# Moving the opening of the sample attention stage into the prompt stick-breaking stage

## The reference

```python
z = einsum('bqhd,blhd->bhql', q, k) * HEAD_DIM ** -0.5 + sb_bias[h]
log_1m = where(k_pos < q_pos, log_sigmoid(-z), 0.0)
suffix = cumsum(log_1m, reverse=True) - log_1m
a = where(k_pos < q_pos, exp(log_sigmoid(z) + suffix), 0.0)
o = einsum('bhql,blhd->bqhd', a, v)
# prompt: 1024 queries on 1024 keys, 4 heads of 64
# samples: 64 queries, each on 4096 keys from a paged pool (page_table) and the new rows
```

## Time and profile before

| | |
|---|---|
| times of three runs | 2071.11, 2075.55, 2075.78 us (median 2075.55) |
| span of the profiled execution, first to last instruction | 2072.7 us |
| its own device time | not among the values given; the span is 1.6 us above the shortest run and 2.9 us below the median |
| PE busy in the span | 1904.4 us (92%) |
| DVE, ACT, POOL busy | 995.9, 591.6, 116.1 us |
| prompt stick-breaking | 642.40 to 776.95 us |
| sample stage | 781.86 to about 1083 us |

### The profile page before, as it was taken

How to read it: one execution, slowest core, us unless ns; L and a number is a source line. 1 busy time by engine, 2 the same in 40 slices (tenths; PEclk the granted TensorE clock), 3 DMA queues, 4 the chain that set the end, 5 groups by cost and what they waited for, 6 DMA issues and landing times. The chain is left out here.

```text
span 2072.7 us, 31712 instructions
## 1 busy us (share of the span) xinstructions
PE 1904.4 (92%) x11702; PEld 1612.2 (78%) x11702; DVE 995.9 (48%) x1976; ACT 591.6 (29%) x982; POOL 116.1 (6%) x210
## 2 busy tenths in 40 slices
PE   7999999998787767888877999999999999999996
PEld 6777779998455444565647889999999999999995
DVE  5213441000573854555548455465555546555547
ACT  4221001111854752333323133221231122123113
POOL 0000000000001101232200001000000000000000
PEclk9999999999787877999988999999999999999998
DMA  5444449311715706999945514221021022102102
GB/s 214 170 165 165 170 170 343 125 54 52 174 14 179 254 1 237 341 344 349 335 181 191 189 37 132 62 61 34 26 61 40 21 60 61 37 23 61 41 11 105
DMA packets 134911, 274.09 MB, mean 132 GB/s; under 512 B 23625, under 2 KB 76506, under 8 KB 130778
## 3 DMA queue, kind: packets, MB, share of 16 engines
q1 hardware_dynamic: 113434, 154.33, 22.5%
q0 software_dynamic: 21376, 118.38, 16.1%
HBM read 243.24 MB, written 78.97 MB: 155 GB/s over the span
## 5 line engine op out<-in xcount | busy, mean ns | idle before, releaser
L2032 DVE TENSOR_TENSOR tl_x<-tl_x,tl_ps 128x512 f32<-128x512 f32 (+1 forms) x198 | 135.0, 686 | 195.6 <-PE tl_ps L2247 192.7
L499 PE MATMUL tl_ps<-tl_T_lo,tl_up_hi 128*128 128x364 f32 (+1 forms) x1008 | 222.3, 329 | 0.0
L499 PE MATMUL tl_ps<-tl_T_hi,tl_up_lo 128*128 128x364 f32 (+1 forms) x1008 | 222.3, 329 | 0.0
L499 PE MATMUL tl_ps<-tl_T_hi,tl_up_hi 128*128 128x364 f32 (+1 forms) x1008 | 222.2, 329 | 0.0
L499 PEld LDWEIGHTS tl_ps<-tl_T_hi,tl_up_hi 128*128 128x128 f32 x1008 | 174.9, 188 | 1.4
L499 PEld LDWEIGHTS tl_ps<-tl_T_hi,tl_up_lo 128*128 128x128 f32 x1008 | 174.8, 188 | 0.0
L499 PEld LDWEIGHTS tl_ps<-tl_T_lo,tl_up_hi 128*128 128x128 f32 x1008 | 174.7, 188 | 0.0
L469 PE MATMUL fr_ps<-fr_w_hi,h_hi 128*128 128x512 f32 x384 | 153.9, 401 | 2.6 <-DVE h_lo L365 2.6
L469 PE MATMUL fr_ps<-fr_w_lo,h_hi 128*128 128x512 f32 x384 | 152.5, 397 | 0.0
L469 PE MATMUL fr_ps<-fr_w_hi,h_lo 128*128 128x512 f32 x384 | 152.4, 397 | 0.0
L2247 PE MATMUL tl_ps<-tl_dn_lo,tl_f_hi 128*128 128x512 f32 x360 | 140.3, 390 | 0.0
(11 more groups left out here) (300 smaller groups left out, 3428.7 us busy)
## 6 DMA issues: line engine op xcount, KB each, us to landing
out_s<-in_cache POOLq DMA_DIRECT2D x8, 4080.0 KB, 20.4
all_lead<-in_w_up SPq DMA_DIRECT2D x44, 512.0 KB, 4.6
fr_raw<-in_w_in POOLq DMA_DIRECT2D x9, 2048.0 KB, 8.8
pg_pages<-in_pool SPq DMA_DIRECT2D x64, 256.0 KB, 4.4
pg_pages<-in_pool POOLq DMA_DIRECT2D x64, 256.0 KB, 4.6
sm_pages<-in_pool POOLq DMA_DIRECT2D x64, 256.0 KB, 4.8
sm_pages<-in_pool SPq DMA_DIRECT2D x64, 256.0 KB, 4.7
zs<-fr_zt SPq DMA_DIRECT2D x48, 256.0 KB, 2.0
```

Source lines behind the costliest of these rows:

```text
L499: last = pe.matmul(out[:, n * 512:n * 512 + b - a], lhs, rhs[:, a:b], start=(i == 0), stop=(i == len(pairs) - 1))
L2032: dve.tensor_tensor(x, x, banks[m % len(banks)][0:n, :], ALU.add).then_inc(added, 1)
```

## The change

The tiles of prompt stick-breaking are taken in the order 0, 4, 6, 7, 5, 3, 2, 1. The rows of all key tiles up to a query tile must then be turned before it: tiles 1 to 4 ahead of query tile 4, tiles 5 and 6 ahead of 6. The buffer `suffix` is dropped; the scan and the exponential work in place in `soft`. `soft`, `odds`, `qk` and `oT` outlive the stage. Their right halves (columns from 512) hold nothing once the last tile of more than 512 keys is done; SP and POOL then load step 2's pages into them. The left halves hold step 3's, loaded when the sample stage begins. The pages no longer have a buffer of their own in the sample stage.

The 64 sample rows are loaded second instead of last. `new_rows`, the softplus of the new rows and `new_sums` run inside iterations -1 to 3 of the prompt stage, in `obank`. Step 0's keys are turned in the last two iterations, through `zbank`. The sample stage keeps step 0's scores and four small loads. The wait for the store of `oT` moves to a late point of the sample stage. The page numbers are read four at a time ahead of four unrolled DMAs instead of in a loop.

```diff
-        PAIRS = [(qt, hp) for qt in range(QT) for hp in range(2)]
+        ORDER = (0, 4, 6, 7, 5, 3, 2, 1)
+        PAIRS = [(qt, hp) for qt in ORDER for hp in range(2)]
+        new_tiles = [range(max(ORDER[:u], default=-1) + 1, qt + 1) for u, qt in enumerate(ORDER)]
+        LONG = max(p for p, (qt, _) in enumerate(PAIRS) if qt >= QT // 2)
...
         @block.sync
+            sp.dma_start(own_rows[:, 0, :], zs[2 * P:3 * P, QB:ZC]).then_inc(row_in[2], 16)
+            sp.dma_start(G["kt"][0:SROWS].rearrange("p u x c -> p (u x c)")[:, 0:ZC], zs[SEQ:ROWS, :]).then_inc(G["rows_in"], 16)
+            for t in range(3, QT):
...
             load_pages(sp, G, a, (0, 1), 0, 2)
+            sp.wait_ge(turned, t_at[LONG, turns[LONG] - 1] + 1)
+            load_pages(sp, G, a, (0, 1), 2, 3)
             sp.wait_ge(o_done, N)
-            sp.dma_start(oTd[:, 2:4, :], oT[:, :, :]).then_inc(o_stored, 16)
-            sp.wait_ge(o_stored, 16)
+            sp.dma_start(oTd[:, 2:4, :], oT[:, :, :]).then_inc(G["o_stored"], 16)
...
         @block.vector
+                if it == 2:
+                    take_sums()
                 for h in range(2):
                     if 0 <= it + 1 < N:
                         scan(2 * it + 2 + h)
+                if it == -1:
+                    pad_new()
+                if it == 0:
+                    bias_new()
+                if it == 1:
+                    sums_new()
+                if it == N - 1:
+                    move_page(dve, 1)
+                    move_page(dve, 3)
+                if it == N:
+                    move_page(dve, 5)
+                    move_page(dve, 7)
...
         @block.tensor
             for it in range(-2, N + 1):
                 if it + 2 < N:
                     if PAIRS[it + 2][1] == 0:
-                        turn_rows(PAIRS[it + 2][0])
+                        for t in new_tiles[(it + 2) // 2]:
+                            turn_rows(t)
                     scores(it + 2)
+                if it == -1:
+                    turn_new()
+                if it == 0:
+                    score_new()
+                if it == 2:
+                    sum_new()
+                if it == N - 1:
+                    turn_pages(0)
+                if it == N:
+                    turn_pages(4)
...
 def load_pages(eng, G, a, groups, first, last, consumed=None):
-                with eng.Fori(0, 4) as j:
-                    page = eng.value_load(G["table"][0:1, ds(j + at, 1)], min_val=0, max_val=NPOOL - 1)
-                    eng.dma_start(pages[:, ds(j + (half + 4 * g), 1), :],
+                of_group = [eng.value_load(G["table"][0:1, at + j:at + j + 1], min_val=0, max_val=NPOOL - 1) for j in range(4)]
+                for j, page in enumerate(of_group):
+                    eng.dma_start(page_group(G, k, g)[:, j:j + 1, :],
...
 def sample_stage(nc, K, G, a, zs, oTd, early):
-            new_rows()
-            turn(0)
             scores(0)
-            new_sums()
-            pe.wait_ge(small_in, 80)
+            pe.wait_ge(small_in, 64)
```

More of the change, by code:

```diff
@@ L918, in _ @@
             extra_pool(pool)
+            pool.wait_ge(turned, t_at[LONG, turns[LONG] - 1] + 1)
+            load_pages(pool, G, a, (2, 3), 2, 3)
         @block.scalar
@@ L970, in _, with pad_new @@
             dve.tensor_scalar(bias_z[:, :], K["bias"][:, :], 1.0 / SCALE, None, ALU.mult).then_inc(bias_done, 1)
+            dve.memset(qpad[:, :, :, :], 0.0).then_inc(zeroed, 1)
             dve.wait_ge(bias_done, 1)
+            def pad_new():
+                dve.wait_ge(zeroed, 1)
+                dve.wait_ge(rows_turned, 2)
+                for j in range(8):
+                    for h in range(2):
+                        part, c = slice(h * HD, h * HD + HD), (2 * (j % 2) + h) * NS
+                        dve.tensor_copy(qpad[part, j, :, c:c + NS],
+                                        obank[part, j * SROWS:(j + 1) * SROWS].rearrange("p (b i) -> p b i", i=NS)).then_inc(padded, 1)
+                dve.tensor_copy(new_kT[:, :, :].rearrange("p j c -> p (j c)"), obank[:, 512:1024]).then_inc(padded, 1)
@@ L1048, in scores, with turn_new, score_new, sum_new @@
                     last.then_inc(z_ready, 1)
+            def turn_new():
+                pe.wait_ge(G["rows_in"], 16)
+                for which, base in enumerate((QA, KA)):
+                    for j in range(8):
+                        c = base + j * P if j < 6 else (QB, KB)[which] + (j - 6) * P
+                        last = pe.transpose(obank[:, which * 512 + j * SROWS:which * 512 + (j + 1) * SROWS],
+                                            new_rows[:, c:c + P], K["ident"][0:SROWS, 0:SROWS])
+                    last.then_inc(rows_turned, 1)
+            def score_new():
+                pe.wait_ge(padded, 17)
+                for hp in range(2):
+                    last = pe.matmul(obank[0:SROWS, 512:512 + wide], new_kT[:, 6 + hp, :],
+                                     qpad[:, 6 + hp, :, :].rearrange("p b c -> p (b c)"), start=(hp == 0), stop=(hp == 1))
+                last.then_inc(new_z_ready, 1)
+            def sum_new():
+                pe.wait_ge(chain_d, 3)
+                pe.matmul(obank[0:SROWS, 768:768 + wide], K["later"][0:SROWS, 0:SROWS],
+                          new_sp[:, :, :].rearrange("p b c -> p (b c)"), start=True, stop=True)
+                pe.wait_ge(spread_done, 1)
+                for b in range(NB):
+                    last = pe.matmul(obank[:, 512 + b:513 + b], spread[:, b, :, :].rearrange("p g c -> p (g c)"),
+                                     K["ones"][0:SROWS, 0:1], start=True, stop=True)
+                last.then_inc(sums_ready, 1)
+            def turn_pages(e0):
+                pe.wait_ge(z_done, 2 * w_at[N])
+                for e in range(e0, e0 + 4):
+                    if e % 2 == 0:
+                        pe.wait_ge(G["page_in"][0][e // 2], 64)
+                    if e >= 4:
+                        pe.wait_ge(page_moved[e % 2], e // 2 - 1)
+                    for j in range(4):
+                        last = pe.transpose(zbank[:, e % 4 * 512 + j * P:e % 4 * 512 + j * P + P],
+                                            page_group(G, 0, e // 2)[:, j, e % 2 * P:e % 2 * P + P], K["ident"][:, :])
+                    last.then_inc(page_turned, 1)
             def turn_weights(p, w):
@@ L1087, in _, with page_group @@
                     values(it - 1, turns[it - 1] - 1)
+def page_group(G, k, g, n=4):
+    u = k % SLOTS
+    if u < 2:
+        return G["pages"][:, u * (PAGES // 2) + 4 * g:u * (PAGES // 2) + 4 * g + n, :]
+    half = slice(512, SEQ) if u == 2 else slice(0, 512)
+    if g < 2:
+        return G["odds"][:, 4 * g:4 * g + n, half]
+    if g == 2:
+        return G["soft"][:, 0:n, half]
+    t = half.start // P
+    return G["qk"][:, t:t + n, :, :].rearrange("p t j c -> p t (j c)")
 def load_pages(eng, G, a, groups, first, last, consumed=None):
     for k in range(first, last):
-        u, half = k % SLOTS, k % 2 * (PAGES // 2)
-        pages = G["pages"][u // 2]
+        u = k % SLOTS
         if k >= SLOTS:
@@ L1121, in sample_stage @@
         STEPS = STICK + NB
[L1122 to L1123 removed]
+        bias_z, fold = G["bias_z"], s.sb("fold", [P, C])
         after, same = s.sb("after", [P, P]), s.sb("same", [P, P])
```

220 lines of the change are left out of this document (104 added, 116 removed).

## The result

The changed kernel took 2057.4 us (median of six executions) beside 2073.84 us for the kernel before on the same chip: 0.9925 of it, with an interval of 0.9909 to 0.994. By the ratio that is 15.6 us less, where the forecast had 5.4 less and a lower end of 2059. That end was drawn around 2075.55 us for before, of which the ratio makes 2060; so the time lies at the edge of the range, and the gain is nearly three times the one forecast. One of the six executions was disturbed (3693 us) and isn't counted in the ratio; the median of the other five is 2056.2 us. The profiled execution took 2055.23 us, its span is 2053.4.

A forecast was written before the change was run, and what follows sets the result against it. The sample stage's steps were taken as set by compute, prompt stick-breaking by a chain through ACT and DVE, with no engine full. Terms -18.2 - 3.5 + 16.3 = -5.4 us took 2075.55 to 2070 us, range 2059 to 2079.

The forecast's parts named there:

- prompt stage: Prompt stick-breaking: the added work and new order make it end 16.3 us later, bounds 9 and 23.
- boundary: Last copy's end to the sample stage: 4.9 us becomes 1.4 without the wait for the oT store, gain 3.5.
- opening: Sample stage's start to the turning of step 1's keys: 23.1 us becomes 5.4, bounds 2.6 and 9.
- head start, first iteration: Step loop's start: step 0's exponentials run before the turning, out of ACT's first move's way; gain 0.5 us (0 to 1.5).
- The fill: Start of prompt stick-breaking: pair 2's scan at 670.3 us, next periods 10.8 and 9.5, priced between half and full clock.
- rival A: Cheap fill: PE at full clock once the big tiles come in prompt stick-breaking; 2064 us, chance 0.25.
- The formula of the periods: Prompt stick-breaking: time between pairs' running sums is scans, leave, exponentials, moves and softplus; later periods together 95.4 us.
- middle periods off the formula: Sign that the forecast is wrong: periods of prompt stick-breaking's middle tiles differ from the summed chain, such as 12.6 and 13.1.
- The order pays nothing by itself: Prompt stick-breaking: a short last tile cuts the 17.6 us drain to 5.6, but periods grow 12.0 us.
- The bound of 9 us: Upper bound for the sample stage's opening: the oT store, 3.9 us, goes in full ahead of the small loads.
- Step 2's and 3's loads, unrolled loads: Page loads: moving them costs nothing; a rival had unrolled issues set the steps' pace, 2086 us, chance 0.10.
- the dear case: Dear fill: half clock up to tile 7 in prompt stick-breaking, 5 to 8 us on top; 2074 us, chance 0.15.

The follow-up runs named there:

- e3: The kernel before with only the unrolled page loads (four page numbers read ahead of four DMAs); 0.9996 of before.
- e5: The changed kernel with the wait for the store of oT back at the end of the prompt stage; 2058.15 us in one run.
- e8: The changed kernel with PE's wait for the four small loads moved behind the turning of step 1; 0.9936 of before.
- e11: The changed kernel again with no edit; 0.9921 of before, median 2057.76 us.
- e6: The changed kernel in tile order 0 to 7, with SP's and POOL's step 2 loads at the sample stage's start; 0.9959 of before.
- e2: The changed kernel with only the tile order set back to 0 to 7; 1.0001 of before.
- e15: The changed kernel in the old tile order, as e2, profiled again; prompt stage 146.6 us, no kernel time given.
- e7: The changed kernel in tile order 0 to 7, with only POOL's step 2 loads moved to the sample stage's start; 2076.57 us in one run.
- e4: The changed kernel with 14 idle transposes on PE ahead of the wait for the new rows; 0.993 of before.
- e12: The changed kernel with tiles 1 and 2 turned ahead of the wait for the new rows, plus e8's edit; 0.9919 of before, median 2055.93 us.

## Why the prediction was wrong, point by point

Means over the profiles (four of before with e3; two of the changed kernel, in the stage four with e5 and e8) against the terms:

| term | forecast | measured |
|---|---|---|
| prompt stage | +16.3 | +11.6 (130.9 to 142.5) |
| boundary | -3.5 | -3.5 |
| opening | -17.7 | -19.3 (24.2 to 4.9) |
| head start, first iteration | -0.5 | -2.0 (12.9 to 10.9) |
| rest of the steps | 0 | -1.1 (271.7 to 270.6) |
| sum | -5.4 | -14.3; by the ratios -15.6 and (e11) -16.4 |

**The step that failed: what the work adds to the prompt stage.** It is 4.7 of the 8.9 us by which forecast and profiles differ; the opening has 1.6, the head start 1.5, the rest of the steps 1.1. The fill was priced between half and full clock, because the row of before had 0.51 up to 666 us. In the changed kernel PE was still at half clock in the first scores of tile 4 and at full clock in the second, and it stayed there through nearly all of the next period (0.98). Pair 2 began 24.5 us into the stage (24.0 to 25.2 in four profiles) instead of 27.9, and the next periods were 9.2, 8.5 and 9.5 instead of 10.8, 9.5 and 10.7. Of the first 3.4 us, some 2.5 are the new rows' scores and the second scores at full clock (1.18, 1.35 and 0.71 us, against 1.97, 2.50 and 1.22 at half). This is rival A's mechanism. I gave it 0.25, and weighed against it a single row; two further profiles of before had 0.80 and 0.81 over that stretch, and e3, whose stage differs only in its page loads, 0.71. By the rule in the Trainium skill (TensorE: Matmul & The Clock Gate, What's actually happening) that sustained busyness releases the engine to 2.4 GHz the fill was this rival, and here it was the better guide. It doesn't order all the rows: the clock was 0.51 with PE busy 20.1 of 24 us in the first profile of before, and 0.62 with 31.1 of 36 in e6.

The clock lies in the base too. The stage that I counted from was 134.5 us long, its repeats 129.0 to 131.0. My 150.9 us for the new stage were 8.4 more than the four profiles' mean, and the base 3.6 more than its own, so that 4.7 are left in the difference. The opening that I counted from was 1.1 us below its own mean, which understated the gain by as much.

**The formula of the periods** was good to 0.8 us behind the fill: 13.1, 13.2 and 12.0 us around the tile of 1024 keys (forecast 13.1, 12.5, 11.2), 8.3 and 7.0 (9.0, 7.7), 5.2, 5.1, 4.1 and 3.4 (5.6, 4.9, 4.3, 3.8), a drain of 8.0 (7.3). The period ahead of them came out at 11.2 for 12.6, and the one before that at 9.5 for 10.7. By the forecast's own sign, middle periods off the formula, it was wrong there; that 11.2 was 11.0 to 12.6 us in nine profiles of the new order with the work, so it isn't a fixed length.

**"The order pays nothing by itself"** was nearly right: 130.4 to 131.3 us against 129.0 to 134.5. What the forecast didn't ask was what the order pays together with the work. The work costs 15.7 us in the old order (130.9 to 146.5 and 146.6) and 11.5 in the new (131.0 to 142.5); before's own spread is as wide as this difference. Of it, some 3.3 us lie in the period into which the new rows' sums fall. In the old order that is one of tile 1, and it grows from 4.3 to 6.3 us to 10.9; in the new one it is one of tile 4, and grows from 7.0 to 9.2. The start up to pair 2 (9.8 us more in the old order, 8.6 in the new) and the drain (2.1 and 1.4) give the rest.

It is tempting to say that the sums are cheap where long operations run beside them, but the clock goes with the order. Over this period it was 0.50 in all four profiles with the work in the old order (e2, e15, e6, e7), and 0.78 to 1.00 in eight of the nine in the new. The ninth is e4, with 0.52, and there the period of tile 4 took 12.5 us, 5.5 more than the 7.0 that it takes at full clock without the sums. In the old order they add 4.6 us to before's 6.3, both at half clock. So their price at half clock is about 5 us in either order, and 2.2 near full clock, which only the new order showed. Whether the order itself brings the clock up wasn't tested.

The order also lets step 2's loads end before the barrier, worth 10 us. I had these loads down as costing nothing, and rightly, but not as something that the order makes so.

**Boundary and opening.** Right in mechanism and size. The mask came in 2.9 us from its issue. The store took 4.0, but it was issued 1.4 us ahead of the sample stage, and landed at 785.7, about when the mask's issue ended. The bound of 9 us had put it in full ahead of the small loads, and that case didn't arise. The opening of before was 25.3 us in half of its profiles (step 0's scores at half clock, 3.64 us), 23.1 in mine.

**Head start.** Consistent with its reason, and four times too small: e8 and e12, which turn step 1 beside the exponentials, have 13.0 and 12.1 us, the changed kernel 10.7 and 11.1.

**Step 2's and 3's loads, unrolled loads.** No wait for a page, and e3 has no effect: right. The 1.1 us in the rest of the steps aren't the unrolling (271.7 in e3); the traces put them down to the clock. In each of the seven profiles of before, e3 and the order alone, one iteration takes 12.8 us in place of 11.1, and PE's clock is at half in it (in before the clock of 857 to 860 us is 0.50). The two profiles of the changed kernel have no such iteration; in the first, the clock falls earlier at the end of the stage instead, which gives back 1.3 us. Why it falls in one kernel and not in the other is open: e8 and e12 have such an iteration too.

**The signs.** Faster by 0.75% had 0.45 in my chances. Ahead of the stage the two first profiles differ by 3.0 us (642.4 and 639.4) without any change in code; over all runs it lies between 638.5 and 647.7. Of the 19.3 us between their spans, 16.7 lie in the stretches that the change touches; the tail was 0.5 longer in the changed kernel.

## What to carry to other kernels

Before a profile's clock goes into a sum, profile the same kernel two or three times: here one stage of one program took 129.0 to 134.5 us, and the row that decided for the dear case was one of several that the clock took. When work is moved into a pipeline, price it at both clocks: here the same sums cost 2.2 us near full clock and about 5 at half. And ask of each load that is started earlier whether it is still under way at the next barrier.

## What the runs showed of the hardware

- The boundary waited for POOL's loads but not for SP's: 11.4 and 11.2 us with POOL's step 2 loads under way (e2, e15), ending 2.3 us behind the last of them, and 1.4 with SP's two of 1 MB under way (e7). In e2 and e7 the store of `oT` took 12.9 and 11.4 us to land, so it isn't the store. Which instruction waits wasn't tried.
- A small load behind large ones in SP's queue: 15.0 us for 256 KB behind 2 MB and the store, with POOL's loads beside it (e7), 2.9 behind the nearly finished store. The Trainium skill (DMA: Bandwidth & Descriptors, Queues, rings and completion order) has descriptors of a queue consumed in ring order on each engine; e7's trace agrees, in which the store and the four small loads behind it landed in the order of their issue. In e6, with the mask ahead of SP's pages and POOL's beside it, it took 6.7.
- The granted clock isn't a property of the program: 0.51, 0.80 and 0.81 over the same instructions. PE's clock long before doesn't order them: in 480 to 560 us the clock was 0.87 ahead of the 0.51, and 0.91 and 0.82 ahead of the 0.80 and 0.81. In the one profile with PE made busy earlier (e4), the stretch at full clock came earlier and ended earlier, as the two windows and the next period (12.5 us instead of 9.2) show.
- A page issue costs SP 0.81 us with page numbers read four at a time ahead of unrolled DMAs, 1.36 in the loop.
